# A hybrid DeltaNet/attention trunk: narrow stationaries and VectorE block turns in the DeltaNet inverse, a half-size weight ring

## What is computed

```python
qkv = jax.nn.silu(causal_depthwise_conv(qkv, conv_w))          # 4 taps
q, k = l2_normalize(q), l2_normalize(k)                        # v as it is
l_mat = jnp.where(strict, einsum('bhnid,bhnjd->bhnij', k_beta, k) * decay, 0.0)
sol = lax.linalg.triangular_solve(l_mat, rhs, left_side=True, lower=True, unit_diagonal=True)
attn_qk = einsum('bhnid,bhnjd->bhnij', q, k) * decay
# per chunk of tokens: v_new = u - w S;  o = q S + attn_qk v_new;  S = S * exp(g) + k v_new
o = rms_norm(o, out_norm_g) * jax.nn.silu(z)
return o @ w_out
```

## Time and profile before

| what | value |
|---|---|
| median of three runs | 2998.84 us |
| the profiled execution, whole | 3000.31 us |
| its span, first to last instruction | 2998.5 us |
| mean granted TensorE clock | 0.982 |
| matmuls busy | 2896.9 us, 97% |
| VectorE, ScalarE busy | 1837.0 us (61%), 1328.9 us (44%) |
| DMA | 493.11 MB, 164 GB/s over the span |

### The profile page before, as it was taken

The page is one execution under the profiler, slowest core; times in us unless marked ns, Lnnn a source line. Parts: engine busy times, 40 slices in busy tenths (PEclk is TensorE's granted clock), DMA queues, the critical chain, the costliest instruction groups (busy, mean ns, idle before and its releaser), DMA issues.

```text
span 2998.5 us, 37768 instructions
## 1 busy us (share of the span) xinstructions
PE 2896.9 (97%) x14080; PEld 2433.9 (81%) x14080; DVE 1837.0 (61%) x2200; ACT 1328.9 (44%) x1539; POOL 26.4 (1%) x29
## 2 busy tenths in 40 slices
PE   7999999999999999999999999889989999999997
PEld 6888888888887788888888878778778888888886
DVE  5777877877777645555555554556655555555555
ACT  6445454453543444444444444544435444444443
POOL 0000000000000000000000000000000000000000
PEclk9999999999999999999999999899999999999999
DMA  6333443434433345555555545532325555555553
GB/s 268 136 131 121 165 150 125 161 131 144 159 114 112 140 183 194 185 194 192 188 194 182 195 176 185 197 113 96 129 85 199 194 191 187 191 189 194 188 190 112
DMA packets 69411, 493.11 MB, mean 164 GB/s; under 512 B 7712, under 2 KB 8032, under 8 KB 10592
## 3 DMA queue, kind: packets, MB, share of 16 engines
q1 hardware_dynamic: 68112, 487.95, 45.4%
q10 hardware_dynamic: 1232, 4.23, 0.4%
HBM read 490.02 MB, written 2.13 MB: 164 GB/s over the span
## 4 chain that ended last, share of the span: by engine, by line
issue 57%; PE 40%; DVE 1%; ACT 1%; POOL 0%; DMA 0%; POOLq 0%; ACTq 0%; SPq 0%; DVEq 0%
PE ACC L483 12%; PE ACC L485 12%; PE ACC L484 12%; PE SIDE L491 2%; PE SIDE L772 1%; PE SIDE L751 0%; PE ACC L714 0%; PE SIDE L789 0%; PE ACC L715 0%; ACT WORK L1091 0%; PE SIDE L769 0%; DVE W_LO L1132 0%; DMA RAW<-stream 0%; PE SIDE L779 0%; DVE WORK L1477 0%
## 5 line engine op out<-in xcount | busy, mean ns | idle before, releaser
L1132 DVE TENSOR_TENSOR W_LO<-RAW,W_HI 128x1024 fp32r<-128x1024 f32 x912 | 1100.0, 1222 | 722.1 <-ACT W_HI L831 716.8
L831 ACT ACTIVATE W_HI<-RAW 128x1024 fp32r<-128x1024 f32 x912 | 961.5, 1059 | 1260.9 <-PE ACC L485 1249.6
L483 PE MATMUL ACC<-W_HI,X_HI 128*128 128x512 f32 x2496 | 992.1, 397 | 15.3 <-DVE W_LO L1132 13.3
L485 PE MATMUL ACC<-W_HI,X_LO 128*128 128x512 f32 x2496 | 975.2, 391 | 0.0
L484 PE MATMUL ACC<-W_LO,X_HI 128*128 128x512 f32 x2496 | 973.7, 390 | 0.0
L483 PEld LDWEIGHTS ACC<-W_HI,X_HI 128*128 128x128 f32 x2496 | 471.1, 189 | 108.8 <-issue 14.0
L485 PEld LDWEIGHTS ACC<-W_HI,X_LO 128*128 128x128 f32 x2496 | 469.8, 188 | 100.3
L484 PEld LDWEIGHTS ACC<-W_LO,X_HI 128*128 128x128 f32 x2496 | 471.0, 189 | 92.6 <-issue 0.6
L483 PE MATMUL ACC<-W_HI,A_HI 128*128 128x512 f32 x1088 | 433.6, 398 | 12.9 <-issue 12.9
L485 PE MATMUL ACC<-W_HI,A_LO 128*128 128x512 f32 x1088 | 426.8, 392 | 0.0
L484 PE MATMUL ACC<-W_LO,A_HI 128*128 128x512 f32 x1088 | 426.3, 392 | 0.0
(11 more groups left out here) (216 smaller groups left out, 1584.2 us busy)
## 6 DMA issues: line engine op xcount, KB each, us to landing
RAW<-stream SPq DMA_DIRECT2D x456, 1024.0 KB, 4.8
WORK<-gdn_rows ACTq DMA_DIRECT2D x8, 512.0 KB, 3.6
WORK<-xt SPq DMA_DIRECT2D x4, 512.0 KB, 9.4
H<-x SPq DMA_DIRECT2D x2, 1024.0 KB, 17.8
out<-WORK SPq DMA_DIRECT2D x4, 512.0 KB, 3.9
WORK<-tails SPq DMA_DIRECT2D x2, 512.0 KB, 12.7
WORK<-gfin SPq DMA_DIRECT2D x1, 1024.0 KB, 6.7
K<-consts SPq DMA_DIRECT2D x1, 678.0 KB, 16.2
```

Source lines behind the costliest of these rows:

```text
L483: nc.tensor.matmul(dst, hi[:, at:at + P], wh, start=first and h % 2 == 0 and q == 0, stop=False)
L485: m = nc.tensor.matmul(dst, lo[:, at:at + P], wh, start=False, stop=last and h % 2 == 1 and q == 1)
L831: nc.scalar.activation(W_HI[:, h % WS, :], raw_piece(h), ACT.Copy).then_inc(hi_ready, 1)
L1132: nc.vector.tensor_tensor(W_LO[:, h % WS, :], raw_piece(h), W_HI[:, h % WS, :].bitcast(f32), SUB).then_inc(lo_ready, 1)
```

## The change

In the inverse, levels 0 to 3 work on the four diagonal blocks of 32 x 32 of each unit. y has 32 stationary columns (the level's masked copy of N's blocks, made once for all levels in the new step `masks`, in `YB`) and so has t (`UQ`, the diagonal blocks of the transpose); each of the 8 matmuls gives 32 rows. Level 4 and 5 have 64 stationary and 64 moving columns. The product u is gone: VectorE turns T's 32 x 32 blocks (`nc.vector.transpose`), ScalarE copies what is needed to `UQ`, `UB` or `UR`. ScalarE takes out y in quadrants of 32 partitions, which move it to the diagonal (`YQ`, zero elsewhere), and t of the last two levels; VectorE subtracts t of the first four in quadrants. ScalarE also makes the conv's tap 3 from PSUM while it takes out qk_t and v_t (VectorE has taps 0 to 2), and the scaling of k_t. The new v has its own home `VN`, the second chunk's q and k have `QK1`. `RAW` has four pieces instead of four chunks, each loaded by a DMA of its own. The tables are written anew. Loads before the first product: the xt blocks and 4 pieces instead of 4 chunks, then as before H, constants and tails.

```diff
 SOLVE_STEPS = gdn_table(SOLVE, """
     0 y0
-    1 t0 u0 conv_v0a
-    2 y1
+    1 t0
+    2 u0 conv_v0a
+    3 y1 conv_v0b
+    4 t1
+    5 u1 conv_v1a y2 strict conv_v1b
+    7 silu_v t2 u2
+    10 y3
+    11 t3 u3
+    13 y4
+    14 t4
+    15 u4 v_t2 y5
+    16 t5 u5 nw
+    18 ru
+    19 v0
+    20 s
+    21 ks
+    22 v1
+    23 o fill
+    24 osum
+    26 oscale
+    30 o_t""")
+LAST_STEPS = gdn_table(SOLVE, """
...
-    13 conv_qk1a
+    1 factors
+    9 dif qk_t
+    10 conv_qk0a
+    11 conv_qk0b conv_qk1a
     15 conv_qk1b
-    16 silu_qk squares
-    17 ss
-    17 decay
-    19 qkn beta
-    20 v_t
-    22 k_t
-    23 kkqk nr
-    26 init""")
+    16 silu_qk
+    18 squares decay ss
+    22 qkn beta
+    23 v_t
+    26 qk1 kkqk k_t
+    27 nr init
+    28 masks""")
...
+    9 qk_t conv_qk0a
+    10 conv_qk0b conv_qk1a
+    11 conv_qk1b
+    15 silu_qk squares
+    17 ss fill qkn factors
+    20 k_t dif v_t
+    21 beta decay kkqk qk1 nr init masks""")
...
-        RAW = sb("RAW", [P, RAWS, CHUNK])
+        RAW = sb("RAW", [P, RAWS, PIECE])
...
-        TR, UR, NR, YR, YC, YD = (sb(n, [P, 1024], f32r) for n in ("TR", "UR", "NR", "YR", "YC", "YD"))
-        Y_OF = [YR] * MASKED + [YC, YD]
+        TR, UR, NR, YQ, YB = (sb(n, [P, 1024], f32r) for n in ("TR", "UR", "NR", "YQ", "YB"))
+        UQ, UB, NQ = sb("UQ", [P, 256], f32r), sb("UB", [P, 512], f32r), sb("NQ", [P, 256])
...
+        def quad_products(p, lhs, rhs):
+
+            for u in range(8):
+                m = nc.tensor.matmul(SIDE[p][0:32, u * P:(u + 1) * P], lhs[:, u * 32:(u + 1) * 32],
+                                     rhs[:, u * P:(u + 1) * P], **ONE)
+            m.then_inc(side_full[p], 1)
+
+        def block_products(p, lv, lhs, rhs):
+
+            for u in range(8):
+                a, b = lhs(u), rhs[:, u * P:(u + 1) * P]
+                dst = SIDE[p][0:64, u * P:u * P + 64]
+                if lv == QUADS:
+                    b = b.rearrange("p (a two n) -> p a two n", two=2, n=32)[:, :, 0, :]
+                    dst = dst.rearrange("p (a n) -> p a n", n=32)
+                else:
+                    b = b[:, 0:64]
+                m = nc.tensor.matmul(dst, a, b, **ONE)
...
+                    pe.wait_ge(n_hi, g + 1)
+                if lv < QUADS:
+                    quad_products(p, YB[:, lv * 256:lv * 256 + 256], TR)
+                else:
+                    block_products(p, lv, lambda u: NR[:, u * P + 64 * (lv - QUADS):u * P + 64 * (lv - QUADS) + 64], TR)
...
+                pe.wait_ge(u_ready, g * STEP_UPS + (lv + 1))
+                if lv < QUADS:
+                    quad_products(p, UQ, YQ)
+                elif lv == QUADS:
+                    block_products(p, lv, lambda u: UB[:, u * 64:(u + 1) * 64], YB)
+                else:
+                    block_products(p, lv, lambda u: UR[:, u * P + 64:(u + 1) * P], YB)
...
-                wait_past(act, conv_done, g * 4 + (2 if name == "v_t" else 0))
-                take_out(act, p, n, cin[:, :, 3:3 + SEQ], SIDE[p][:, :].rearrange("p (b n) -> p b n", n=SEQ))
+                nth, dst = (1, cv) if name == "v_t" else (0, cq)
+                wait_past(act, conv_done, g * 4 + 2 * nth)
+                wait_past(act, qkn_done, g + nth)
+                if nth == 0:
+                    nc.scalar.activation(CW[:, :], PRM[:, ds(g * 32 + A_CONV, 32)], ACT.Copy).then_inc(cw_ready, 1)
+                act.wait_ge(side_full[p], n)
+                nc.scalar.activation(cin[:, :, 3:3 + SEQ], SIDE[p][:, :].rearrange("p (b n) -> p b n", n=SEQ), ACT.Copy)
+                act.wait_ge(cw_ready, g + 1)
+                for b in range(4):
+                    wc = CW[:, 16 * nth + 4 * b + 3:16 * nth + 4 * b + 4]
+                    at = slice(b * SEQ, (b + 1) * SEQ)
+                    i = nc.scalar.activation(dst[:, at], SIDE[p][:, at], ACT.Copy, scale=wc)
+                i.then_inc(side_out[p], 1)
...
+                for r in range(4):
+                    i = nc.scalar.activation(units(NQ[:, :], 32)[32 * r:32 * r + 32, :, :], quad(N, r), ACT.Copy)
+                i.then_inc(nc_done, 1)
...
+                if lv < QUADS:
+                    for r in range(4):
+                        i = nc.scalar.activation(quad(YQ[:, :], r), quad(SIDE[p][:, :], 0, r), ACT.Copy)
+                elif lv == QUADS:
+                    for q in range(2):
+                        i = nc.scalar.activation(quad(YB[:, :], 2 * q + 1, 2 * q), quad(SIDE[p][:, :], q), ACT.Copy)
+                else:
+                    i = nc.scalar.activation(band(YB[:, :], 2, 64)[:, :, 0:64], band(SIDE[p][:, :], 0, 64)[:, :, 0:64],
+                                             ACT.Copy)
...
+                act.wait_ge(u_turned, g * LEVELS + (lv + 1))
+                if lv < QUADS - 1:
+                    for r in range(4):
+                        i = nc.scalar.activation(units(UQ[:, :], 32)[32 * r:32 * r + 32, :, :], quad(UF, r), ACT.Copy)
+                elif lv == QUADS - 1:
+                    nc.scalar.activation(UB[:, :].rearrange("p (u a n) -> p u a n", a=2, n=32), odd(units(UF)), ACT.Copy)
+                    i = nc.scalar.activation(UR[:, :], UF, ACT.Copy)
...
-                        i = nc.vector.tensor_scalar(d, src, wc, None, MUL)
-                    else:
-                        i = nc.vector.scalar_tensor_tensor(d, src, wc, d, MUL, ADD)
-                if tap < 3:
+                    i = nc.vector.scalar_tensor_tensor(d, src, wc, d, MUL, ADD)
+                if tap < 2:
...
+            elif kind == "t" and lv < QUADS:
                 dve.wait_ge(side_full[p], n)
-                nc.vector.tensor_tensor(units(YR[:, :]), units(side[:, :]), every(K_LV + lv * P), MUL)\
-                  .then_inc(side_out[p], 1)
-            elif kind in ("t", "u"):
-                buf, cols = (TR, 0) if kind == "t" else (UR, 1)
-                dve.wait_ge(side_full[p], n)
-                part = halves(buf[:, :], lv, cols)
-                nc.vector.tensor_tensor(part, part.bitcast(f32), halves(side[:, :], lv, cols), SUB)\
-                  .then_inc(side_out[p], 1)
+                for r in range(4):
+                    part, w_ = (quad(buf, *at).rearrange("p u (a two n) -> p u a two n", two=2, n=2 << lv)[:, :, :, 0, :]
+                                for buf, at in ((TR[:, :], (r, r)), (side[:, :], (0, r))))
+                    i = nc.vector.tensor_tensor(part, part.bitcast(f32), w_, SUB)
+                i.then_inc(side_out[p], 1)
+            elif kind == "u":
+                gdn_done(dve, f"t{lv}", it)
+                t_ = TR[:, :].bitcast(f32)
+                if lv < QUADS:
+                    i = nc.vector.transpose(UF, t_)
+                for r, c in {4: ((1, 0), (3, 2)), 5: ((2, 0), (2, 1), (3, 0), (3, 1))}.get(lv, ()):
+                    i = nc.vector.transpose(quad(UF, c, r), quad(t_, r, c))
+                i.then_inc(u_turned, 1)
...
+            load_piece(0, 0)
+            load_piece(0, 1)
             load_xt(1)
-            load_chunk(1)
+            load_piece(1, 2)
+            load_piece(1, 3)
...
             for k in range(RAWS):
-                sp.wait_ge(lo_ready, 2 * k + 2)
-                load_chunk(RAWS + k)
-                if k == 0:
-                    sp.dma_start(K[:, K_EARLY:], consts[:, K_EARLY:]).then_inc(in_masks, 16)
+                sp.wait_ge(lo_ready, k + 1)
+                load_piece(2 + k // 2, RAWS + k)
+            sp.dma_start(K[:, K_EARLY:], consts[:, K_EARLY:]).then_inc(in_masks, 16)
 
             def feed(first, end):
-                with sp.Fori(first // RAWS, end // RAWS) as i:
+                with sp.Fori(2 * first // RAWS, 2 * end // RAWS) as i:
                     for k in range(RAWS):
-                        sp.wait_ge(lo_ready, i * 2 * RAWS + 2 * (k - RAWS + 1))
-                        sp.dma_start(RAW[:, k, :], stream[i * RAWS + k]).then_inc(raw_full[k], 16)
-
-            feed(2 * RAWS, B_KV + 8)
+                        sp.wait_ge(lo_ready, i * RAWS + (k - RAWS + 1))
+                        load_piece(i * (RAWS // 2) + k // 2, k)
```

209 lines of the change are left out of this document (100 added, 109 removed).

## The result

The changed kernel takes 2969.76 us (median of four, 2967.61 to 2976.46), the kernel before 2998.06 beside it: ratio 0.991, 95% interval 0.9895 to 0.9926. I forecast 2935, with 2908 to 2968. The direction was right; the gain was 28 us where I had 64, and the time lies above the range. The profiled execution has a span of 2966.3 us against 2998.5, so it is 32.2 us that the two traces have to explain.

What follows compares the result with a forecast made beforehand. TensorE, busy 97% of the span, was taken to bound the kernel. Gains of 38 (passes 2 to 6), 13 (passes 1 and 7), 10 (last solve) and 3.8 (first group), less 0.5, made 64.3 us off 2998.84: 2935, range 2908 to 2968.

Steps and rivals of the forecast that it cites:

- the ring: Prefetch of weight pieces, now four places: in steady state each refill lands before it is due, so no cost.
- passes 1 and 7: The two DeltaNet loop passes with fewer weight pieces: 6.5 us gained in each, 13 together.
- the last solve: The final inverse, where the chain between engines decides: t0 to nw falls from 46.0 to 36.3 us; 10 gained altogether.
- The price of a small step: Narrow y or t step of eight matmuls on TensorE: 0.46 us against 0.84, because the stationary load is the limit.
- The loop's passes: DeltaNet passes 2 to 6: 9.9 us less TensorE work, 2.3 of stalls, so 7.6 gained each, 38 together.
- The start: First loads, with pieces 4 to 7 queued behind H, constants and tails: about 0.5 us lost, between 0 and 4.
- The first group: The first group's waits for normalised q/k and a split mostly go, kkqk waits 2.8: about 3.8 us gained.
- The clock: Sign of a wrong forecast: TensorE's granted clock, 1.00 in a pass, showing 1.2 GHz inside passes 2 to 6.
- No stalls: Rival: no new waits in the loop's passes, 8 x 9.9 plus gains at both ends, 85 us: 2914; chance 0.17.
- slower: Rival: VectorE's 32-bit transpose at a quarter rate, 4.9 us each, stalls every pass: about 3020; chance 0.07.
- Narrow is not cheaper: Rival: narrow matmul pairs have a floor, so only the u products' removal gains, 36 us: 2963; chance 0.13.
- dearer: Rival: VectorE transposes at 2.4 us or quadrant pieces at 0.5, costing 28 us over the passes: 2964; chance 0.13.

Runs made afterwards that it cites:

- the second profile: The changed kernel run again without any edit, profiled a second time beside the other runs: 2971.63 us, ratio to the kernel before 0.9915.

## Why the prediction was wrong

The forecast failed in terms, not in its picture of the loop. The term put at nothing, the ring, is the step that took the time out of the range: with eight places it is 2959 us, inside it. The terms for passes 1 and 7 and for the last solve were too large, and hold 16 of the 32.1 us between forecast and trace; the ring holds 6.9 in attention.

**The price of a small step: right.** I took 0.46 us, the trace has 0.43 to 0.52, and the run with one side wide shows that the stationary side was the reason. The Trainium skill, "TensorE: Matmul & The Clock Gate", section "Back-to-back issue gap", gives about 81 ns for a pair whose matmul moves 128 columns, without saying how many are loaded; here it is 60 with 32 loaded columns. The Trainium skill's section "LDWEIGHTS (loading the stationary operand)" on the same page, columns over 1.2, makes an estimate of 27 ns for 32 columns; the trace's load record lasts 108 ns, but eight pairs go by in 0.48 us, so the array time left of it is at most 60.

**The loop's passes: right in mechanism, 0.7 us a pass off.** The two waits I walked out came at t3 (1.1 us) and nw (1.0), and all idle time of a pass is 2.27 us where I had 2.3. The 0.7 are in TensorE's own work: it fell from 120.0 to 110.9 us and not to 110.1. The twelve narrow steps take 5.96 us together and not 5.5, the other small steps 0.1 more than before and the 32 pieces 0.15 more. The transposes took 1.24 us each (I had 1.2), the t pieces 0.28 (0.29), and a y in quadrants 1.51 to 1.53, a u 1.7 (1.55 for both). My remark that neither engine is full was right; that ScalarE's standing in front of a transpose is what made t3 wait was in the walk ("1.7 of waiting for u2's"), and it was the part that could be had back.

**The ring: the step that failed.** "In steady state ... nothing" compared the time to refill a place with pieces of 2.74 us, the DeltaNet's pace. I did not look at the stretch where pieces go fastest: in attention splits follow one another at 0.95 us at the closest. There four places are emptied sooner than they are filled. It cost 8.9 us in the trace (6.9 with the 2.0 that the clock gave back); the ring as a whole 10.5 between the medians. My own sign of failure, splits that wait for the stream after the first 30 us, came. The start cost 2.1 instead of 0.5: I had the fifth piece's data at 21.7 us and the piece ready at 24.1; its split began at 23.7, TensorE with it at 26.15.

**Passes 1 and 7: present waits were counted that are not theirs.** I added the new waits at ru to o (5.1) to the loop's 2.3 and subtracted 4.2 of present ones. The new waits came about as large. The table of waits for pass 7 after begins

```profile
PE SIDE L546 <- ACT WORK L876: 2.1, 1, 2.1
PE SIDE L546 <- ACT TR L1025: 1.1, 1, 1.1
PE SIDE L546 <- DVE NR L1409: 1.0, 1, 1.0
```

where the first is v0 behind ss (I had a wait of 2.4 at s), and in all TensorE idles 7.6 us in pass 7 (I had 7.4) and 9.6 in pass 1, where 2.8 more stand at a piece near its end. But before the change these passes idled only 2.5 and 1.9 us. The stretch 807 to 927 of the earlier trace rows, from which I took 4.2, idles 5.1, and 3.1 of that is behind 909.69, in the last solve: the waits at 915.24 and 923.88 of the earlier trace rows. The other part of the miss is TensorE's own work, which I had at 9.9 less. It fell by 9.9 and 9.7 us in the second profile, at a granted clock of 1.00, and by 8.3 and 8.4 in the first, at 0.98. With 1.9 for 4.2, pass 7 comes to 9.7 - 7.6 + 1.9 = 4.0 us, and the second profile has 4.1. The passes gained 1.2 to 2.8 and 2.7 to 4.1 us in the two profiles; in the run with eight places pass 1 took 104.0, longer than before the change, at a granted clock of 0.95.

**The last solve: the chain was counted short.** I had 7.4 us for a level with a split; t0 to t1 to t2 to t3 are 8.9, 8.9 and 9.4, and before they were 8.6, 8.3 and 7.0 (the second from 923.88 to 932.16, the third to 939.12). The change made each TensorE step half as long, but put a transpose and two sets of quadrant copies where one mask and one subtraction had been. My working had all of these durations; it left out that t0 came late because VectorE still had masks, a sum and splits of the pass before, that ScalarE does two splits in some levels, and the low clock. I had 36.3 us for t0 to nw; it took 46.1 and 48.9. The order of the copies accounts for 3 to 5 of the difference, since 43.4 came without it; how the rest divides is not shown.

**The first group: a wait was moved, not removed.** I wrote that the sums of squares come after the gates' transfer and that perhaps 1 us was left. The 5.5 us of the earlier trace rows are gone, and there is

```profile
PE SIDE L600 <- ACT WORK L966: 4.2, 1, 4.2
```

in their place, since silu and squares went behind the gates in ScalarE's row, and the granted clock from 72 to 80 us, behind that wait, is 0.59. kkqk waits 2.8 as I had said.

**The clock** was in my text only as a sign of failure inside passes 2 to 6, where it stayed at 1.00. At both ends some waits are followed by slow products. In the changed kernel from 904 to 912 us, behind the waits at t3 and y4:

```profile
904.00:912.00 8.00, 6.59 (x28) 5.07 (x28) 3.23 (x8) 4.67 (x7) 0.00 (x0) 0.57 0.39 131
```

The Trainium skill's page "TensorE: Matmul & The Clock Gate", section "Part 1: The HAM clock gate (the "warmup" mystery)", says of a kernel's start that the count of slow matmuls differs between runs of one kernel. Here it is so in the middle of one: behind the same t5 the first profile has none and the second twelve.

**The rivals.** "No stalls" and "slower" did not come. "Narrow is not cheaper" (2963) and "dearer" (2964; its own sum, 28 on top of 2935, is 2963) lie nearest in time and are refuted by the traces: a narrow step takes 0.48 us, a transpose 1.24, a quadrant 0.28 on VectorE and 0.37 to 0.42 on ScalarE. They have about the right size for a wrong reason. The range was too narrow because all its cases shared the same terms for the ring and for the ends.

## What to carry to other kernels

A prefetch ring is sized by the stretch that empties it fastest, not by the one with the most work; look for that stretch before halving it. When you subtract waits that stand there now, read them from the stretch itself and not from one that overlaps its neighbour. Where the engine with the most work idles at several places of a stretch, much of its savings there turns into new waits until the chain of the others is shorter: write that chain out, step by step, in the order of each engine's own row. And when one engine waits for another inside its row, look first for work of its own that can stand in the wait; here that brought 0.9 us a pass, while moving the step that was late cost 2.8.

## What the runs showed of the hardware

- A matmul with 32 or 64 stationary columns followed the last after 54 to 70 ns, one with 128 after 102 to 112, with 64 or 128 columns moving over it.
- VectorE's 32-bit transpose of 128 x 1024 in blocks of 32 x 32 takes 1.24 us, as its other passes over as many elements here (1.21 to 1.28); one of 32 x 256 takes 0.44 us, against 0.28 for a subtraction of 32 x 128.
- After waits of 2.81 and 2.65 us at the same step, a piece ran at 2.4 GHz in one execution of a kernel and at 1.2 GHz in another, 2.8 against 5.3 us. That is most of the 2.6 us by which their last solves differ.
- In the wait at the start the stream brought one piece of 512 KB every 1.3 us (404 GB/s from 23.5 to 27.5 us); where it is asked for one place at a time, as in attention, splits began 1.2 to 3.3 us apart (266 GB/s from 1877 to 1899 us).
